# Where VectorE scales a chunk's output in a gated-delta and attention kernel: third level of the next inverse, or after the eleventh attention slot

## The reference, cut to what matters

```python
u = triangular_solve(a_mat, vc * bc[..., None]); w = triangular_solve(a_mat, kb * exp(gc)[..., None])
def step(state, xs):
    v_new = u_i - einsum('bhcd,bhde->bhce', w_i, state)
    o_i = einsum('bhcd,bhde->bhce', q_i, state) + einsum('bhij,bhje->bhie', a_i, v_new)
    state = state * gl_i[..., None, None] + einsum('bhcd,bhce->bhde', k_i, v_new)
    return state, o_i
...
o_dn = rmsnorm(o_dn.astype(x.dtype), g_dn_out) * silu(z_dn)
```

## Time and profile before

| | us |
|---|---|
| median of 3 runs | 4284.16 |
| lowest, highest | 4273.37, 4284.92 |
| the profiled execution | 4278.54 |
| its span | 4276.8 |
| PE busy | 3653.6 (85%) |
| DVE busy | 1489.8 (35%) |
| ACT busy | 1146.6 (27%) |
| POOL busy | 816.9 (19%) |

### The profile page before, as it was taken

One profiled execution on the slowest core, in us unless ns is written; L12 is line 12 of the kernel. 1 busy time (PEld: TensorE's weight loads), 2 busy tenths in 40 slices (PEclk: granted clock), 3 DMA queues, 4 the chain that ended last, 5 costly groups with the idle time before them and its releaser, 6 DMA issues. The chain is left out here.

```text
span 4276.8 us, 58938 instructions
## 1 busy us (share of the span) xinstructions
PE 3653.6 (85%) x23914; PEld 3476.2 (81%) x23914; DVE 1489.8 (35%) x1892; ACT 1146.6 (27%) x2073; POOL 816.9 (19%) x428
## 2 busy tenths in 40 slices
PE   7998999598888888846784999999999699997786
PEld 6998998387777777745783999999999689887785
DVE  6451222255555555634386000000000133331443
ACT  4111211255544554510222101101011233331322
POOL 3001111111111111111310111110110344443222
PEclk9999999589889898975896999999999899998898
DMA  3223343422333233173343334211110545543310
GB/s 110 61 70 79 138 152 142 148 70 67 80 78 73 64 86 85 49 189 86 128 158 149 131 118 159 96 45 53 39 59 30 171 155 175 169 139 115 125 66 37
DMA packets 266019, 443.05 MB, mean 104 GB/s; under 512 B 55763, under 2 KB 209171, under 8 KB 250308
## 3 DMA queue, kind: packets, MB, share of 16 engines
q1 hardware_dynamic: 265868, 440.79, 32.5%
HBM read 300.13 MB, written 174.14 MB: 111 GB/s over the span
## 5 line engine op out<-in xcount | busy, mean ns | idle before, releaser
L78 PE MATMUL pd_prod<-pd_h_hi,pd_whi 128*128 128x412 f32 x1760 | 615.8, 350 | 34.1 <-DVE pd_h_lo L2258 34.1
L79 PE MATMUL pd_prod<-pd_h_hi,pd_wlo 128*128 128x412 f32 x1760 | 617.0, 351 | 0.0
L80 PE MATMUL pd_prod<-pd_h_lo,pd_whi 128*128 128x412 f32 x1760 | 616.9, 351 | 0.0
L78 PE MATMUL pa_proj<-pa_h_hi,pa_whi 128*128 128x412 f32 x1160 | 410.5, 354 | 53.1 <-DVE pa_h_lo L408 24.3
L79 PE MATMUL pa_proj<-pa_h_hi,pa_wlo 128*128 128x412 f32 x1160 | 409.5, 353 | 0.0
L80 PE MATMUL pa_proj<-pa_h_lo,pa_whi 128*128 128x412 f32 x1160 | 408.1, 352 | 0.0
L2267 DVE TENSOR_TENSOR pd_act<-pd_prod,pd_gate 128x412 f32<-128x412 f32 x110 | 64.5, 586 | 909.8 <-PE pd_prod L80 909.8
L78 PE MATMUL pe_prod<-pe_ahi,pe_whi 128*128 128x412 f32 x880 | 317.1, 360 | 72.2 <-POOL pe_wlo L2370 40.1
L78 PEld LDWEIGHTS pd_prod<-pd_h_hi,pd_whi 128*128 128x128 f32 x1760 | 331.9, 189 | 38.1 <-issue 29.8
L79 PEld LDWEIGHTS pd_prod<-pd_h_hi,pd_wlo 128*128 128x128 f32 x1760 | 332.1, 189 | 2.2
L80 PEld LDWEIGHTS pd_prod<-pd_h_lo,pd_whi 128*128 128x128 f32 x1760 | 331.7, 188 | 1.4
(11 more groups left out here) (353 smaller groups left out, 6291.4 us busy)
## 6 DMA issues: line engine op xcount, KB each, us to landing
pe_w<-in_w_down SPq DMA_DIRECT2D x80, 704.0 KB, 4.1
scratch_at<-pa_work SPq DMA_DIRECT2D x24, 1024.0 KB, 5.6
pb_qkv<-scratch_at SPq DMA_DIRECT2D x32, 768.0 KB, 7.3
scratch_a<-pd_act SPq DMA_DIRECT2D x22, 1030.0 KB, 5.3
pe_a<-scratch_a SPq DMA_DIRECT2D x5, 4532.0 KB, 21.3
pd_w<-in_w_gate_up SPq DMA_DIRECT2D x44, 512.0 KB, 5.9
out_new_cache_k<-in_cache_k SPq DMA_DIRECT2D x8, 2046.0 KB, 11.1
out_new_cache_v<-in_cache_v SPq DMA_DIRECT2D x8, 2046.0 KB, 16.3
```

The costliest lines, as they stand in the source:

```text
L78: pe.matmul(out, w_hi, a_hi, start=first, stop=False)
L79: pe.matmul(out, w_lo, a_hi, start=False, stop=False)
L80: return pe.matmul(out, w_hi, a_lo, start=False, stop=last)
```

## The change

`finish(c - 1)` on DVE leaves level 3 and is put behind slot 10, ahead of the wait for the product with the state (`p1_done`) and the making of `vnew`. Nothing else is moved, added or removed on any engine; the programs of PE, ACT, POOL and SP are the same.

```diff
                     m.then_inc(xt_sub, 1)
-                    if level == 3 and not first:
-                        finish(c - 1)
                     if level < IN_HALF:
                         dve.wait_ge(x_done, c * (LEVELS - 2) + level)
                         dve.tensor_tensor(X[:, :], X[:, :], half_bank(2), ALU.subtract).then_inc(x_sub, 1)
                 slot(c, par, jj, 10)
+                if not first:
+                    finish(c - 1)
                 dve.wait_ge(p1_done, c + 1)
                 dve.wait_ge(u_copied, c + 1)
                 dve.tensor_tensor(vnew[:, :], U[:, :], bank(3), ALU.subtract).then_inc(vnew_done, 1)
```

## The result

| | us |
|---|---|
| before, median of 4 runs | 4278.76 |
| after, median of 4 runs | 4339.82 |
| lowest and highest after | 4338.41, 4353.76 |
| ratio after to before, 95% interval | 1.0153 (1.0126 to 1.0179) |
| profiled execution after, its span | 4340.74, 4338.9 |

The changed kernel is 61 us slower. The first line of the page after, beside the earlier trace rows: PE does the same work, and its share of a longer span is smaller.

The account below looks back on a forecast made before the run. PE, busy 85% of the span, was taken to bound the kernel, with DVE mattering only where PE waits behind it. The terms -31.1 + 46.4 + 45 + 0 gave +60 us, so 4341 us, range 4295 to 4386.

Parts of the forecast that it names:

- The pause at level 4: Level 3, the old place: PE's pause ahead of level 4's first product goes in 15 chunks, saving 31.1 us.
- The wait at `vnew`: Slot 10, the new place: `vnew` on DVE starts 3.09 us late in 15 chunks, costing 46.4 us.
- The queue behind the moved step: Chunk borders: SP's transfers go out later, so DVE waits for `uo_free` at slot 0; +45 us.
- The clock: TensorE's granted clock behind old and new pauses: taken as even, zero, with ends of -49 and +50 us.
- The signs: Expected profile: no level 4 pause, `vnew` 3.1 us later, even borders 13 to 14 us, SP or DMA releasing DVE.
- (B): Only the exchange of places counts, no queue wait at the borders: +15 us, 4294 to 4300 us, chance 0.10.
- (C): The clock behind level 4's pause gives back all 49 us, new pauses leave it alone: 4270 to 4276, chance 0.09.
- (D): Next raw rows load late behind `uo` stores, so ACT's squares and PE's norms wait: 4367 to 4390 us, chance 0.19.

## Why the prediction was right, and where it wasn't

The forecast was 4341 us and slower; measured were 4339.82 us and +1.5%. By its own steps:

**The pause at level 4, -31.1 us: right in kind, too small.** The row of it is gone, and chunk 0 had shown how PE runs there without it. But I had read the 11 short pauses, 5.4 us, as standing at other levels and staying. They stood at the next product behind level 4's, had the same cause, and went too: 36.5 us.

**The wait at `vnew`, 15 times 3.09 us, +46.4 us: right.** The waits say 46.7 us in 15 times, and the cut says +46.4.

**The queue behind the moved step, +45 us: the mechanism right in kind, wrong in one link, too small in size.** With SP's transfers freed 61 us come back, with unit 0's load freed 57. At the eight even borders the store of `uo[0]` lands 9.8 us after its issue on the mean, where I had 10.0, and `uo_free` comes some 13.6 us after `vnew`, as worked out. The step that failed is the sentence that PE's wait for unit 0's load "ends earlier and lies inside" DVE's wait for `uo_free`. It ends earlier, by 0.9 us on the mean, but PE's transposes and scores come behind it and take 1.8 to 3.2 us more before DVE can start, so this path ends last, 0.9 to 2.3 us behind `uo_free`. As the two end so close together, the size at these borders came out near all the same: 37.2 us (123.4 - 86.2), where I had 35. That is luck in part. At the six odd borders the step failed altogether: I had taken the back edge's pause as room in which the queue's wait would be hidden, and the pause itself grew to between 3.3 and 8.6 us. That is 25.6 us of waiting (39.0 - 13.4), in a term that I had put at 10.

**The clock, zero with ends of -49 and +50: mis-sized.** Both halves were real and not even. The old pause had cost some 39 us in the clock (76 us in run time with the step in level 2, less 36.5 of pauses). The new pause at slot 11 costs 27 us in the kernel with SP freed and 19 us in the one with the dummy reciprocal, less than the 37 I had put for it and the border pauses together. The kernel with SP freed shows the rest: it is 1.9 us slower than before (4278.78 - 4276.84), and -36.5 of pauses, +46.4 of late `vnew` and +5.5 at the back edge leave -13.5 us for the clock. The queue then has the other 61 us, and the 5.5, against the +45: the total is right in part because the misses cancel.

**The signs.** No pause at level 4, `vnew` 3.1 us later, and SP's store 1.69 us behind the scaling came as written. The even borders take 13.6 to 19.4 us, 15.4 on the mean, not 13 to 14, and PE and not SP releases DVE there. The granted clock from the first `vnew` to the last is 0.89 before and after. It didn't move as a mean, but it did in place: the even borders went from 1.00 to between 0.72 and 0.88, and the stretch from level 3 to `vnew`, 0.67 to 1.00 before, to between 0.87 and 1.00.

**The rivals.** (B) needed the queue to be harmless; it isn't. (C), the clock decides, was right about what the old pause cost, and wrong that the new ones would leave the clock alone and that this could decide: the queue alone takes back more. (D), ACT late with the squares: there is no such wait in the profile after. The raw rows that (D) speaks of land 24 to 31 us after `vnew`, where (D) had 33.7 and ACT wants them at 31.6; slot 0 to level 3 lost only 6.9 us in 15 chunks.

## What to carry to other kernels

Before a step is moved to a later place, look for what its semaphore releases on the engine that issues the transfers: everything behind that wait is moved too, past every point at which the next stage needs it. A step that delays a bounding engine by 2 us can cost twice that, through the clock behind the pause; the place to look for is one where the engine is idle while the bounding engine works on things that don't need it, as level 2 was here: 4 us of DVE work cost nothing there, and the kernel became 1.6% faster than before. Where two waits end within 1 or 2 us of each other, a run that frees one of them says little; look first whether the edit frees it at all, as the run with `uo[0]`'s store early did not.

## What the runs showed of the hardware that I had not expected

A loop's back edge on PE is a point at which DMA traffic counts, whatever the data: a pause of 2.1 to 2.5 us with idle DMA engines was 3.3 to 8.6 us with the kernel's own burst in them, and 3.5 to 4.8 us with three dummy loads of 768 KB.

A pause of PE of about 2.2 us in a stretch of small products (64x64), with the short one behind it, cost 2.4 us in itself and 2.6 us in the granted clock behind it, on the mean of 15 chunks; a pause of 2.3 us at slot 11, with larger products behind it (128x128), cost 1.3 us in the clock, and one of 3.1 us there 1.8 us (27 us over 15, the kernel with SP freed). That the two differ is measured, why isn't.
